# Gate columns made as part of the first mLSTM value rows, with a block of a convolution projection in each row

## The reference, cut to what matters

```
proj = hn @ w_in                                 # 512 x 1024 @ 1024 x 4112
pa, pb = proj[..., :A_COLS], proj[..., A_COLS:]
qkv  = silu(causal_conv(pa[..., :1536], conv_w)) # 12 blocks of 128 columns: q, k, v of 4 heads
beta = sigmoid(pa[..., 1536:1540])               # gates of A, 4 columns
g    = -exp(a_log) * softplus(pa[..., 1540:1544] + dt_bias)
vb   = pb[..., 1024:1536]                        # mLSTM values, 4 heads of 128
i_log = pb[..., 1536:1540] + i_bias              # gates of B, 8 columns
f_log = log_sigmoid(pb[..., 1540:1544] + f_bias)
```

## Time and profile before

| | |
|---|---|
| median of 3 executions | 3087.88 us (3084.46 to 3088.75) |
| span of the profiled execution, first to last instruction | 3080.7 us |
| PE busy | 3051.1 us, 99% of the span |
| granted PE clock over the span | 1.000 |
| DVE, ACT, POOL busy | 37%, 41%, 56% |
| weight panels | 1002, of 256 KB |

### The profile page before, as it was taken

One profiled execution on the slowest core, in us unless ns is written; L12 is line 12 of the kernel. 1 busy time (PEld: TensorE's weight loads), 2 busy tenths in 40 slices (PEclk: granted clock), 3 DMA queues, 4 the chain that ended last, 5 costly groups with the idle time before them and its releaser, 6 DMA issues.

```text
span 3080.7 us, 40589 instructions
## 1 busy us (share of the span) xinstructions
PE 3051.1 (99%) x15246; PEld 2503.3 (81%) x15246; DVE 1126.3 (37%) x2098; ACT 1253.4 (41%) x2278; POOL 1718.0 (56%) x1358
## 2 busy tenths in 40 slices
PE   9999999999999999999999999999999999999999
PEld 8888877887777788778888878888888887788887
DVE  5322321223666523223222586633111358221214
ACT  4322332333455535443333343345333457643334
POOL 6555655565554466455555633357555664665554
PEclk9999999999999999999999999999999999999999
DMA  5333323322222234333333322123333332233332
GB/s 168 99 95 96 100 68 89 91 84 72 81 74 66 79 105 122 83 95 98 97 96 96 88 61 59 46 76 96 93 99 100 99 86 56 76 99 93 96 108 87
DMA packets 149840, 275.24 MB, mean 89 GB/s; under 512 B 16528, under 2 KB 17808, under 8 KB 149520
## 3 DMA queue, kind: packets, MB, share of 16 engines
q1 hardware_dynamic: 149648, 272.66, 31.4%
HBM read 270.50 MB, written 2.10 MB: 88 GB/s over the span
## 4 chain that ended last, share of the span: by engine, by line
PE 94%; DVE 4%; issue 1%; ACT 1%; POOL 0%; DMA 0%; SPq 0%; DVEq 0%; ACTq 0%; POOLq 0%
PE PS L835 91%; PE PS L909 2%; DVE AR L1465 1%; PE PS L902 1%; DVE PS L1465 0%; DVE TMP L1471 0%; DVE AR L1471 0%; ACT AR L2262 0%; DMA RAW<-in_wst 0%; DVE PS L1471 0%; DVE SM L1764 0%; DVE SM L1468 0%; DVE TMP L1465 0%; POOL TMP L2662 0%; SPq L2807 0%
## 5 line engine op out<-in xcount | busy, mean ns | idle before, releaser
L2662 POOL TENSOR_TENSOR WL<-RAW,WH 128x512 fp32r<-128x512 f32 x1001 | 1295.1, 1307 | 816.8 <-ACT WH L2262 816.4
L2262 ACT ACTIVATE WH<-RAW 128x512 fp32r<-128x512 f32 x1002 | 617.6, 628 | 970.7 <-PE PS L835 901.0
L835 PE MATMUL PS<-HH,WH 128*128 128x512 f32 x2264 | 893.0, 394 | 3.8 <-ACT AR L2262 2.2
L835 PE MATMUL PS<-HL,WH 128*128 128x512 f32 x2264 | 881.6, 389 | 1.0 <-DVE HL L1471 1.0
L835 PE MATMUL PS<-HH,WL 128*128 128x512 f32 x2264 | 882.4, 390 | 0.0
L835 PE MATMUL PS<-AH,WH 128*128 128x512 f32 (+1 forms) x1504 | 581.6, 387 | 2.0 <-DVE AL L1465 1.2
L835 PE MATMUL PS<-AL,WH 128*128 128x512 f32 (+1 forms) x1504 | 578.9, 385 | 2.3 <-DVE AL L1465 2.3
L835 PE MATMUL PS<-AH,WL 128*128 128x512 f32 (+1 forms) x1504 | 578.6, 385 | 0.0
L835 PEld LDWEIGHTS PS<-HH,WH 128*128 128x128 f32 x2264 | 425.3, 188 | 96.0 <-issue 5.7
L835 PEld LDWEIGHTS PS<-HH,WL 128*128 128x128 f32 x2264 | 424.9, 188 | 90.4 <-DVE WL L1465 0.4
L835 PEld LDWEIGHTS PS<-HL,WH 128*128 128x128 f32 x2264 | 425.4, 188 | 87.5 <-DVE HL L1471 2.0
(11 more groups left out here) (240 smaller groups left out, 2453.3 us busy)
## 6 DMA issues: line engine op xcount, KB each, us to landing
RAW<-in_wst SPq DMA_DIRECT2D x1002, 256.0 KB, 2.7
X<-in_x SPq DMA_DIRECT2D x8, 256.0 KB, 5.9
TMP<-in_p SPq DMA_DIRECT2D x8, 256.0 KB, 3.3
out<-X SPq DMA_DIRECT2D x8, 256.0 KB, 2.0
AR<-in_dm SPq DMA_DIRECT2D x1, 1024.0 KB, 4.9
AR<-in_mem SPq DMA_DIRECT2D x1, 1024.0 KB, 7.9
CST<-in_cst SPq DMA_DIRECT2D x1, 612.0 KB, 5.8
AR<-in_pos SPq DMA_DIRECT2D x2, 256.0 KB, 3.5
```

The source lines that it names most:

```text
L835: return e.matmul(o, l, r, start=a, stop=z, skip_group_check=True)
L2262: return e.activation(o, a, f, **kw)
L2662: return e.tensor_tensor(o, a, b, op)
```

## The change

- `ab_gl` and `ab_gt` are gone on PE and DVE.
- Each `m_v` 0, k row streams 272 weight columns in place of 256: the sixteen gate columns are a third, short block. The gates arrive on token partitions in columns 256 to 271 of the four value banks.
- Each such row also does one block, three matmuls of 512 columns, of `c` 1, 1, so that a row uses one whole panel of four blocks. Step `c` 1, 1 then has nothing left on PE. Its bank is taken at the first row.
- `gv` 0 on DVE now waits for the last row and for the factor, scales the gates out of the four banks into SR with four `tensor_scalar` of 128 x 16, and goes on as before. ACT's value copies wait for these four.
- In `PLAN`, `gv` 0 and `gv` 1 stand behind `m_v` 0, 7, followed by `fq` 0, `c` 1, 1 and `gs`. Their entries in `LATE` are dropped.
- `tok_row` takes a list of column lists; its other callers pass the same columns as before through `side`.

```diff
 def plan_ab():
-    p += [("fac", "na"), ("ab_gl",), ("bc", "na"), ("ab_gt",), ("gv", 0), ("c", 0, 1), ("m_v", 0, 0), ("m_v", 0, 1), ("m_v", 0, 2),
+    p += [("fac", "na"), ("bc", "na"), ("c", 0, 1), ("m_v", 0, 0), ("m_v", 0, 1), ("m_v", 0, 2),
...
-        ("ab_open", 3), ("ab_open", 4), ("c", 0, 1), ("ab_open", 5), ("ab_open", 6), ("ab_open", 7), ("fac", "nfin"), ("fac", "na"), ("ab_gl",),
-        ("bc", "na"), ("m_v", 0, 0), ("m_v", 0, 3), ("m_v", 0, 4), ("gv", 0), ("ab_gt",), ("c", 0, 0), ("m_v", 0, 5), ("c", 0, 2), ("m_v", 0, 1),
-        ("m_v", 0, 2), ("gv", 1), ("m_v", 0, 6), ("fk", 0), ("m_v", 0, 7), ("fq", 0), ("c", 1, 1), ("gs",), ("c", 1, 0), ("n", 0), ("dec", 0),
+        ("ab_open", 3), ("ab_open", 4), ("c", 0, 1), ("ab_open", 5), ("ab_open", 6), ("ab_open", 7), ("fac", "nfin"), ("fac", "na"),         ("bc", "na"), ("m_v", 0, 0), ("m_v", 0, 3), ("m_v", 0, 4), ("c", 0, 0), ("m_v", 0, 5), ("c", 0, 2), ("m_v", 0, 1),
+        ("m_v", 0, 2), ("m_v", 0, 6), ("fk", 0), ("m_v", 0, 7), ("gv", 0), ("gv", 1), ("fq", 0), ("c", 1, 1), ("gs",), ("c", 1, 0), ("n", 0), ("dec", 0),
...
     LATE: vector ("gv", 0): 3 and ("gv", 1): 1 and scalar ("gv", 0): 6 are dropped
...
-            def tok_row(outs, k, name, l, col, ncol, opd, first, last, done=None):
+            def tok_row(outs, k, name, l, tiles, ncol, opd, first, last, done=None):
-                ws = [block(name, l, [(128 * k, 1, 128)], [(col + 128 * j, 1, 128)]) for j in range(ncol // 128)]
+                ws = [block(name, l, [(128 * k, 1, 128)], cols) for cols in tiles]
...
-                elif kind == "ab_gl":
-                    lin(("ab_gl",), ("ab_gl",), "w_in_ab_2", 0, [(1536, 1, 8), (3592, 1, 8)], range(8))
-                elif kind == "ab_gt":
-                    o = bank("ab_gates")
-                    e.wait_ge(*at("ab_gl"))
-                    for t in range(4):
-                        z = e.transpose(o[:, 16 * t:16 * t + 16], tmp(6)[0:16, 128 * t:128 * t + 128], CST[0:16, C_ID:C_ID + 16])
-                    z.then_inc(*up("mm", "ab_gt"))
...
-                    if h:
+                    if h and (h, j) != (1, 1):
                         lin(("c", h, j), ("tap", h, j, 3), "w_in_ab_2", 0, cc(512 * j + 128 * h), range(8))
...
                     if k == 0:
                         opened[kind] = [bank("m_v", p, t) for t in range(4)]
-                    tok_row(opened[kind], k, "w_in_ab_2", 0, BOFF + 1024 + 256 * p, 256, "H", k == 0, k == 7, ("m_v", p) if k == 7 else None)
+                        if p == 0:
+                            opened["c"] = bank("tap", 1, 1, 3)
+                    tiles = side(BOFF + 1024 + 256 * p, 2) + ([[(1536, 1, 8), (3592, 1, 8)]] if p == 0 else [])
+                    tok_row(opened[kind], k, "w_in_ab_2", 0, tiles, 256 if p else 272, "H", k == 0, k == 7, ("m_v", p) if k == 7 else None)
+                    if p == 0:
+                        w = block("w_in_ab_2", 0, [(128 * k, 1, 128)], cc(512 + 128))
+                        z = mm3(opened["c"], w, HH[:, k, :], HL[:, k, :], k == 0, k == 7)
+                        if k == 7:
+                            z.then_inc(*up("mm", "c", 1, 1))
...
-                elif kind == "ab_gt":
-                    e.wait_ge(*at("mm", "ab_gl"))
-                    tt(tmp(6)[0:16, :], psum("ab_gl")[0:16, :], RB[0:16, :], MUL).then_inc(*up("ab_gl"))
-                    e.wait_ge(*at("mm", "ab_gt"))
-                    e.tensor_copy(SR[:, :, :], psum("ab_gates")[:, 0:64].rearrange("p (t c) -> p t c", t=4)).then_inc(*up("ab_gates"))
                 elif kind == "gv" and i[0] == 0:
                     src = SR[:, :, :]
-                    e.wait_ge(*at("ab_gates"))
+                    e.wait_ge(*at("mm", "m_v", 0))
+                    e.wait_ge(*at("factor", "na"))
+                    for t in range(4):
+                        ts(SR[:, t, :], psum("m_v", 0, t)[:, 256:272], nr("na")[:, t, 0:1], None, MUL).then_inc(*up("ab_gates", t))
+                    e.wait_ge(*at("ab_gates", 3))
...
-                    e.wait_ge(*(at("mm", "m_num", 1) if p else at("factor", "na")))
+                    e.wait_ge(*(at("mm", "m_num", 1) if p else at("ab_gates", 3)))
```

More of the change, by code:

```diff
@@ L275, in plan_ab @@
     p = [("ab_open", k) for k in range(4)] + [("fac", "nfin")] + [("ab_open", k) for k in range(4, 8)]
-    p += [("fac", "na"), ("ab_gl",), ("bc", "na"), ("ab_gt",), ("gv", 0), ("c", 0, 1), ("m_v", 0, 0), ("m_v", 0, 1), ("m_v", 0, 2),
-          ("c", 0, 0), ("m_v", 0, 3), ("m_v", 0, 4), ("m_v", 0, 5), ("c", 0, 2), ("m_v", 0, 6), ("m_v", 0, 7), ("gv", 1), ("f", 0), ("c", 1, 1), ("gs",), ("n", 0), ("c", 1, 0), ("dec", 0),
+    p += [("fac", "na"), ("bc", "na"), ("c", 0, 1), ("m_v", 0, 0), ("m_v", 0, 1), ("m_v", 0, 2),
+          ("c", 0, 0), ("m_v", 0, 3), ("m_v", 0, 4), ("m_v", 0, 5), ("c", 0, 2), ("m_v", 0, 6), ("m_v", 0, 7), ("gv", 0), ("gv", 1), ("f", 0), ("c", 1, 1), ("gs",), ("n", 0), ("c", 1, 0), ("dec", 0),
           ("m_q", 0), ("f", 1), ("LT", 0), ("c", 1, 2), ("n", 1), ("gr", 0), ("dec", 1), ("at", 0), ("m_k", 0), ("LT", 1), ("gr", 1), ("m_og", 0),
@@ L616 @@
         ("g", 1, 1): 2, ("d_q", 7, 1): 2, ("d_pv", 0): 1, ("d_t2", 2): -2, ("d_sc", 4, 3): -1, ("g", 1, 3): -3, ("d_t2", 4): -3, ("g", 1, 5): 2,
-        ("m_w", 0): 2, ("c", 0, 2): 9, ("f_down", 1, 5, 3): 5, ("c", 2, 2): 2, ("gv", 0): 6, ("f_down", 1, 5, 5): 2, ("uu", 1): 1,
+        ("m_w", 0): 2, ("c", 0, 2): 9, ("f_down", 1, 5, 3): 5, ("c", 2, 2): 2, ("f_down", 1, 5, 5): 2, ("uu", 1): 1,
         ("f_down", 1, 5, 7): 5, ("l", 0, 6, 0): -1, ("m_og", 0): 10, ("m_fin", 1): -3, ("f_down", 1, 5, 2): 1, ("m_w", 1): 6, ("f_down", 1, 5, 4): 3,
@@ L916, in spread @@
                 turned(label, done, lambda t: r[:, t, col:col + 1].to_broadcast([128, 128]), NORM[n][3])
+            side = lambda c, n: [[(c + 128 * j, 1, 128)] for j in range(n)]
             cc = lambda c0, n=128: [(c0, 1, n)]
@@ L979, in tensor @@
                         opened[kind] = [bank("r_v", h, t) for t in range(4)]
-                    tok_row(opened[kind], k, "w_in", 0, O_RV + 512 * h, 512, "H", k == 0, k == 7, ("r_v", h) if k == 7 else None)
+                    tok_row(opened[kind], k, "w_in", 0, side(O_RV + 512 * h, 4), 512, "H", k == 0, k == 7, ("r_v", h) if k == 7 else None)
                 elif kind == "r_sc":
@@ L1109, in tensor @@
                         opened[kind] = [bank("mv", g, t) for t in range(2)]
-                    tok_row(opened[kind], k, "mem_w_kv", 0, 1024 + 512 * g, 512, "A", k == 0, k == 7, ("mv", g) if k == 7 else None)
+                    tok_row(opened[kind], k, "mem_w_kv", 0, side(1024 + 512 * g, 4), 512, "A", k == 0, k == 7, ("mv", g) if k == 7 else None)
                 elif kind == "ms":
@@ L1411, in tensor @@
                         opened[kind] = [bank("sv", t) for t in range(4)]
-                    tok_row(opened[kind], k, "w_qkv_c_2", 0, 1280, 256, "H", k == 0, k == 7, ("sv",) if k == 7 else None)
+                    tok_row(opened[kind], k, "w_qkv_c_2", 0, side(1280, 2), 256, "H", k == 0, k == 7, ("sv",) if k == 7 else None)
                 elif kind == "sr":
```

## The result

Before: 3087.67 us, median of 9 runs. After: 3094.06 us, median of 9 runs (3092.32 to 3097.79). The ratio is 1.0025, with a 95% interval of 1.0016 to 1.0034: 7.7 us slower (5 to 10.5). The median lies 0.6 us from the forecast and inside its range. The ratio lies on the slower side of the bound of 0.2%, where I had put 0.36 and not the larger chance; its interval reaches over the bound to both sides.

What follows compares the result with a forecast made beforehand. PE, busy 99% of the span, was taken as the bound. Less work, newly uncovered waits and wider rows summed to +3.6 us, with 2.0 us of slow clock +5.6: from 3087.88 to 3093.5 us, range 3087.5 to 3098.5 us.

Steps and rivals of the forecast that it cites:

- the bound of 0.2%: On the whole time, 6.2 us either way counts as no change; chances: slower 0.36, same 0.61, faster 0.03.
- Removed and added work: On PE, 5.9 us go with `ab_gl` and `ab_gt`; widening the `m_v` rows to 272 columns adds 0.64 us.
- What `ab_gl` was hiding: Before `bc` na, PE now waits 3.2 us for POOL's factor; rows start 1.68 us behind `bc`, at 1756.8.
- The gate chain, uncovered: Before `gs`, PE waits about 8 us for the gates; `gs` starts at T + 9.2, 3.6 us later than before.
- Restarting after the wait: Behind the wait before `gs`, PE runs at half rate for about 4 us, losing 2 us (bounds 0 and 3.5).
- the sum: All terms for this place together: +3.6 us, or +5.6 us with 2.0 us of slow clock.
- rival C: The clock falls twice, also around `bc`, slowing the first `m_v` rows by another 2 to 3 us: 3096 us; chance 0.15.
- A: As summed: both covers gone, the clock falls once; 3093.5 us, range 3091 to 3096; chance 0.45.
- The granted clock: At the program's start the trace shows 1.00 despite slower matmuls, read as a lower clock level the view does not show.

Runs made afterwards that it cites:

- e4: e3 plus 12 matmuls that nobody reads ahead of `bc` na, in its wait for the factor; median 3088.02 us, ratio 1.0004.
- e3: The changed kernel with 32 matmuls of 512 columns that nobody reads put ahead of `gs`; median 3088.68 us, ratio 1.0009.
- e8: The changed kernel with `c` 1, 1 again its own pass behind `fq` 0, each row's fourth block loaded but unused; median 3085.45 us, ratio 1.0000.
- e10: e9 with ACT's and POOL's panel conversions capped from the last value row until `gs`; median 3085.54 us, ratio 0.9991.
- e11: e10 with 12 matmuls that nobody reads in `bc`, while PE waits for the factor; median 3084.41 us, ratio 0.9991.
- e13: e10 with the cap on panel conversions two panels lower; median 3083.95 us, ratio 0.9988.
- e9: e8 with DVE's order changed: `fk` 0 ahead of `gv` 0, `fq` 0 behind `gv` 1; median 3087.15 us, ratio 0.9999.
- e6: The changed kernel with DVE's order alone changed: `fk` 0 before the gates, `fq` 0 behind them; median 3088.82 us, ratio 1.0008.
- e12: e6 with ACT and POOL converting no panel beyond a cap from the last value row until `gs`; median 3090.69 us, ratio 1.0011.

## Why the prediction came out as it did

- *Removed and added work*: right. 272 columns start 125 ns apart (126.7 forecast), a row takes 2.19 us (2.20).
- *What `ab_gl` was hiding*: right as to the waits. `bc` starts at 1754.78 after 2.86 us (forecast 1755.1), and the wait for the copy to RBT is there again, 1.12 us. But the rows start 2.24 us behind `bc` and not 1.68, at 1757.02 (1756.8), because the transposes already run at half rate.
- *The gate chain, uncovered*: right. The last row ends at T = 1776.90, and `gs` starts at T + 8.79 (T + 9.2 forecast), a wait of 8.19 us (8.1). DVE and POOL of the changed kernel:

```profile
1778.35 0.66 DVE L1466 TENSOR_SCALAR SR<-PS,SM 128x16 f32<-128x16 f32 x4
...
1781.69 1.21 DVE L1466 TENSOR_SCALAR Z<-Z 128x32 f32<-128x32 f32 x1
1782.93 2.01 DVE L1469 SCALAR_TENSOR_TENSOR Z<-Z 128x32 f32<-128x32 f32 x9
```

```profile
1781.60 1.26 POOL L2659 TENSOR_TENSOR WL<-RAW,WH 128x512 fp32r<-128x512 f32 x1
```

  The scalings took 0.66 us and not 0.45; the 0.45 came from a copy of another form. One operation of `gv` 1 is over 1 us, next to one POOL panel, as forecast; it costs 1.04 us, not 1.2.
- *Restarting after the wait*: the mechanism was right, the term too small: 2.0 us in the sum, 2.8 measured.
- *The step that failed* is in rival C, "Against it: the gap is broken by the transposes, and shorter than the second". The gap of 2.86 us was long enough by itself: the clock fell in it, at about 1754.1, before the transposes began. They took 1.11 us in place of 0.60 and the first row 4.05 us (1757.02 to 1761.07) in place of 2.19, and e4 against e3 puts 2.5 us on both. The sum had nothing for this. C, at 0.15, is what happened; A, at 0.45, is not.
- *The granted clock*: the prediction took from the earlier trace rows that this view need not show a fall. In the changed kernel it shows both.

The place so cost 3.2 us for the waits net of the work saved (forecast 3.6) and 5.0 us for two falls (forecast 2.0): 8.2 us, where I had 5.6 and C had 8.1. That the median is yet within 1 us of the forecast is partly luck: it is a difference of 6.4 us between medians of executions that scatter by several us, and the ratio says 5 to 10.5. Besides, the sum was worked out on an execution at a mean clock of 1.000 and then added to a median that holds some falls already; of the 7.2 us between the two, 2.5 us lie outside the span and 4.7 us are such scatter. That I held "within 0.2%" likeliest has the same root: with two falls the forecast would have been 3096 us, beyond the bound.

The half of the change that did the harm is the joining of `c` 1, 1, in so far as it left nothing between the last row and `gs`. Undoing it alone (e8) brought the ratio from 1.0025 to 1.0000, 7.7 us, as much as I had expected. The ledger has only 3.5 us for it, but its row is e8's longest execution (3091.18 us, where the median is 3085.45), so the size of this step is not well known. What the trace does show is that the wait stayed 1 to 3 us longer than expected: a pass of `lin` in that place frees panels, whose conversion on POOL holds the chain. With that treated too (e10, e11, e13) the ratios go below 1, and only in e13 clear of it.

## What to carry to other kernels

Before taking work off the engine that is busy 99%, look at what waits it covers, and count for each uncovered wait both the wait and a slow restart behind it: here waits of 2.9 and 8.2 us each brought one. Work moved to cover a wait brings its own followers with it (here the panel conversions that its weights set off, and the wait that it used to cover), so give each its place by hand. Of a chain of tiny DVE operations, look at each one's duration against its usual one: one that is far above it and ends together with a POOL operation may be held by POOL. Here holding the panels back won 2.0 us. And before reading a gain off one trace, compare that execution's time and mean clock with those of the kernel's other executions.

## What the runs showed of the hardware that I had not expected

- A single wait of 2.9 us was enough to lower the clock. Ten traces leave the wait for the factor open (2.86 to 2.88 us), and in all ten the granted clock fell, between 0.9 us before `bc` started and 2.0 us after. In e4 and e11, with 12 matmuls in this wait, it stayed at 1.00. Nor does it take a second wait behind the transposes: in e8, e9, e10 and e13 the rows follow `bc` at once. PE in e10:

```profile
1754.22 0.65 PE L906 MATMUL PS<-CST,SM 128*128 128x128 f32 x4 [2.87 <-POOL SM L2657]
...
1755.12 0.43 PE L832 MATMUL PS<-WH,HL 128*128 128x272 f32 x1
1755.35 0.43 PE L832 MATMUL PS<-WH,HH 128*128 128x272 f32 x1
```

- A wait of the same length can do either. Before, 2.04 us in front of `gs` were followed by starts 227 ns apart; in e13, 2.07 us by seven or eight at 427 ns, from the third or fourth matmul on. What tells the two apart no run here shows. Most executions of the kernel before do have some fall (mean clock 0.998 or 0.999, the traced one 1.000), and it may be here. That would explain why, except for the changed kernel itself, every kernel's ratio is some 2 to 5 us better than its ledger. Where they fall is open.
- Small falls come and go elsewhere, whatever the kernel. The same stretch in the changed kernel, then in e6, whose list for PE is the same:

```profile
1880.00:1900.00 20.00, 19.89 (x102) 17.55 (x103) 9.95 (x21) 5.83 (x9) 3.10 (x3) 0.91 0.01 1
```

```profile
1880.00:1900.00 20.00, 20.00 (x100) 16.90 (x99) 10.77 (x21) 5.26 (x10) 5.05 (x4) 1.00 0.20 53
```

  The time from `n` 0 to the end of the span is 1294.3 us in e6 and in the kernel before, 1297.1 to 1297.4 us in the changed kernel, e3, e8, e9, e11 and e12, and 1299.0 us in e4. That is a good part of the scatter between executions, and the reason for the ledger.
- POOL holds some DVE operations and not others. In e10 the four scalings out of PSUM (SR<-PS, 1768.90) took 0.66 us as always, while POOL was in two panels from 1767.22 to 1769.75; operations from SBUF to SBUF that met a panel were held, by up to 1.1 us (1.27 us in place of 0.17 in e13). POOL's short operation on 128 x 4 held none there: in the changed kernel it ran from 1780.62 to 1781.63, and the DVE operations in that time took 0.17 to 0.42 us as in the kernel before. The Trainium skill ("SBUF — State Buffer", section "SBUF: two separate sides") has it that POOL and certain DVE operations exclude each other for a whole instruction; the trace agrees, with 2.00 us against 4.02 us for the same nine operations.
- At the start of the program the view still gives 1.00 for the slower pace. Here the same column reads 0.57 and 0.71 where matmuls start at half rate, so the column does report falls, and why it doesn't there stays open.
